# A decoder step's output and gate stages in 512-column chunks, with three row tiles per weight slice

## The reference, cut to what matters

```
o = concat([oa, ob], axis=-1) @ w_out                      # (rows, 2048) @ (2048, 2048)
x = x + _rmsnorm(o, post_w)                                # mean of squares over all 2048 columns
x = x + sigmoid(x @ w_pg + b_pg) * (p @ w_pe)              # gate (2048 x 2048), per-layer input p (256 wide)
```

## Time and profile before

| | us |
|---|---|
| three runs | 4167.61, 4165.46, 4152.4 (median 4165.46) |
| span of the profiled execution | 4170.6 |
| the stage's first matmul to its last | 3133.4 to 4166.0 |
| of these: seven output chunks | 411.0 |
| eighth output chunk, norm and turning | 85.2 |
| eight gate chunks | 536.4 |

### The profile page before, as it was taken

How to read it: one execution, slowest core, us unless ns; L and a number is a source line. 1 busy time by engine, 2 the same in 40 slices (tenths; PEclk the granted TensorE clock), 3 DMA queues, 4 the chain that set the end, 5 groups by cost and what they waited for, 6 DMA issues and landing times. The chain is left out here.

```text
span 4170.6 us, 54158 instructions
## 1 busy us (share of the span) xinstructions
PE 3649.0 (87%) x19483; PEld 2868.8 (69%) x19513; DVE 1942.5 (47%) x3408; ACT 685.9 (16%) x1533; POOL 709.4 (17%) x722
## 2 busy tenths in 40 slices
PE   5969797989898888879789789989979999999999
PEld 3657484857575656658475378778868888888887
DVE  2038686868688989888945311111110000411111
ACT  4010202121111112121200022222220000400000
POOL 2015161615152433325100200000000000000000
PEclk8979798989798988979799879999989999999999
DMA  9865665655565555555510110110040110401012
GB/s 356 249 199 171 206 194 195 205 195 179 199 192 186 186 187 173 163 176 174 187 30 11 46 46 26 35 42 26 6 145 27 40 40 21 136 23 45 23 45 81
DMA packets 355974, 507.28 MB, mean 122 GB/s; under 512 B 58529, under 2 KB 275898, under 8 KB 354546
## 3 DMA queue, kind: packets, MB, share of 16 engines
q1 hardware_dynamic: 312240, 352.67, 27.1%
q0 software_dynamic: 39552, 142.63, 9.8%
q10 hardware_dynamic: 3922, 8.65, 0.5%
HBM read 470.74 MB, written 33.14 MB: 121 GB/s over the span
## 5 line engine op out<-in xcount | busy, mean ns | idle before, releaser
L961 PE MATMUL Z<-W,hT 128*128 128x256 f32 x4096 | 916.6, 386 | 33.2 <-DMA W<-in_w_in_dram 19.7
L961 PEld LDWEIGHTS Z<-W,hT 128*128 128x128 f32 x4096 | 790.1, 194 | 155.4 <-issue 45.7
L1884 PE MATMUL Z<-W,hT 128*128 128x256 f32 x2048 | 456.1, 381 | 4.3 <-PE DB L1895 2.3
L1817 PE MATMUL Z<-W,hT 128*128 128x256 f32 x2048 | 446.9, 381 | 1.3 <-ACT small L1946 1.3
L1884 PEld LDWEIGHTS Z<-W,hT 128*128 128x128 f32 x2048 | 390.6, 191 | 61.1 <-issue 7.7
L1817 PEld LDWEIGHTS Z<-W,hT 128*128 128x128 f32 x2048 | 389.4, 191 | 57.3 <-issue 4.5
L714 POOL TENSOR_TENSOR kprod<-kib,qib 128x256 f32<-128x256 f32 x256 | 348.9, 1372 | 408.1 <-ACT small L802 196.2
L1008 PE MATMUL DB<-big,ex 128*4 128x256 f32 x2048 | 181.8, 488 | 85.8 <-DMA big<-in_cache_diff_v_dram 85.4
L738 POOL DMA_DIRECT2D big<-in_cache_diff_v_dram x256 | 136.4, 533 | 666.3 <-PE DB L1008 533.2
L865 DVE MAX8 small<-big 128x8 f32<-128x512 f32 (+1 forms) x256 | 245.2, 958 | 5.9 <-DVE small L871 1.2
L866 DVE MATCH_REPLACE8 big<-small,big 128x512 f32<-128x512 f32 (+1 forms) x256 | 241.2, 942 | 0.0
(11 more groups left out here) (471 smaller groups left out, 4229.4 us busy)
## 6 DMA issues: line engine op xcount, KB each, us to landing
big<-in_cache_diff_k_dram SPq DMA_DIRECT2D x256, 512.0 KB, 4.3
big<-in_cache_diff_v_dram POOLq DMA_DIRECT2D x256, 512.0 KB, 5.3
W<-in_w_in_dram SPq DMA_DIRECT2D x29, 2048.0 KB
W<-in_w_in_dram SPq DMA_DIRECT2D x48, 1024.0 KB, 7.3
W<-in_w_out_dram SPq DMA_DIRECT2D x8, 2048.0 KB, 8.1
W<-in_w_ple_gate_dram SPq DMA_DIRECT2D x8, 2048.0 KB, 8.4
kib<-in_cache_idx_k_dram SPq DMA_DIRECT2D x256, 32.0 KB
W<-in_x_prompt_dram SPq DMA_DIRECT2D x16, 512.0 KB
```

Source lines behind the costliest of these rows:

```text
L961: mm = pe.matmul(Z[c % 2][:, 0:CW], hT[:, k, t * P:(t + 1) * P], W[:, s, k, :], start=(k == 0), stop=(k == KT - 1))
L1817: mm = pe.matmul(Z[t % 2][:, 0:CW], hT[:, k, t * P:(t + 1) * P], W[:, s, k, :], start=(k == 0), stop=(k == KT - 1))
L1884: pe.matmul(Z[b][:, 0:CW], hT[:, k, t * P:(t + 1) * P], W[:, 1 - s, k, :], start=(k == 0), stop=(k == KT - 1))
```

## The change

- A chunk is now `NQ` = 512 columns: four chunks for each of the two products. Each matmul fills a whole PSUM bank.
- A chunk is done in three groups of three row tiles (`GROUPS`): 0, 1, 2; then 3, 4, 5; then sample rows, 6, 7. Inside a group, the loop over `k` is outside and that over the three row tiles inside. Two sets of three banks (`BANKS`, made of `S` and `Z`) alternate; `TB` and `DB` serve the turning and the per-layer input.
- The weights are a ring of four slices of four `k` (1 MB each). A slice is loaded again as soon as group 2 has used it.
- VectorE takes the tiles out of PSUM, ScalarE squares each 512-column piece at once. Scale and residual go in pieces of 512, in the last three groups of the output part; the residual rows have buffers of their own.
- Tiles 0 to 2 are turned after group 1 of the last output chunk, 3 to 5 after its group 2, the rest after the first group of the gate part.
- Gate: the per-layer matmuls of a group stand in the next group at `k` 3, 6 and 9. Results are stored chunk by chunk. The last group of the program (`last_group`) goes tile by tile.
- The loops of the stage are written out instead of being hardware loops.

```diff
@@ the heads' stage, sync: the first chunk of w_out
-                for c in range(2):
-                    sp.dma_start(W[:, c, :, :], wo[:, :, c * CW:(c + 1) * CW]).then_inc(h_next, 16)
+                for q in range(2):
+                    sp.dma_start(W[:, q, :, :].rearrange("p b c -> p (b c)").rearrange("p (k n) -> p k n", n=512),
+                                 wo[:, 8 * q:8 * q + 8, 0:512]).then_inc(h_next, 16)
@@ the output and gate stage
-        NCO = D // CW
+        NQ = 512
+        NCO = D // NQ
...
+        GROUPS = ((0, 1, 2), (3, 4, 5), (NT, 6, 7))
+        ORDER = ((0, 1, 2), (3, 4, 5), (6, 7, NT))
+        BANKS = ((S[0][:, 0:NQ], S[0][:, NQ:2 * NQ], S[1][:, 0:NQ]), (S[1][:, NQ:2 * NQ], Z[0][:, :], Z[1][:, :]))
+        SIDE = (TB[:, :], DB[:, :])
+        NG = 2 * NCO * 3
...
+                def slices(C, q):
+                    src = (wo if C < NCO else wg)[:, 4 * q:4 * q + 4, (C % NCO) * NQ:(C % NCO) * NQ + NQ]
+                    if C:
+                        if q < 3:
+                            sp.wait_ge(o_wu[q], C)
+                        else:
+                            sp.wait_ge(o_z, 9 * C)
+                    sp.dma_start(Wr[:, 4 * q:4 * q + 4, :], src).then_inc(o_w[q], 16)
+                def residual(n):
+                    t, c = n // 4, n % 4
+                    if n >= 4:
+                        sp.wait_ge(o_xm, n - 3)
+                    src = xp[:, t, c * NQ:(c + 1) * NQ] if t < NT else xs[:, c * NQ:(c + 1) * NQ]
+                    sp.dma_start(xq[c][0:rows(t), :], src).then_inc(o_x[c], 16)
...
+                def store(c, g):
+                    for j, t in enumerate(ORDER[g]):
+                        sp.wait_ge(e_y, 9 * c + 3 * g + j + 1)
+                        dst = yp[:, t, c * NQ:(c + 1) * NQ] if t < NT else ys[:, c * NQ:(c + 1) * NQ]
+                        sp.dma_start(dst, oq(t, c)).then_inc(e_st, 16)
...
+                for C in range(1, NCO):
+                    for q in range(4):
+                        slices(C, q)
+                for n in range(4 * 3):
+                    residual(n)
+                for q in range(2):
+                    slices(NCO, q)
+                for n in range(4 * 3, 4 * 6):
+                    residual(n)
+                for q in range(2, 4):
+                    slices(NCO, q)
+                for n in range(4 * 6, 4 * (NT + 1)):
+                    residual(n)
+                gate_vectors(0)
+                gate_vectors(1)
+                for c in range(NCO):
+                    store(c, 0)
+                    if c + 1 < NCO:
+                        slices(NCO + c + 1, 0)
+                        slices(NCO + c + 1, 1)
+                    store(c, 1)
+                    if c + 1 < NCO:
+                        slices(NCO + c + 1, 2)
+                        slices(NCO + c + 1, 3)
+                    store(c, 2)
+                    if c + 2 < NCO:
+                        gate_vectors(c + 2)
...
+                def one(gi, t, k):
+                    mm = None
+                    if k == 0 and gi >= 2:
+                        pe.wait_ge(o_zf, 3 * (gi - 2) + ORDER[gi % 3].index(t) + 1)
+                    b = bank(gi, t)
+                    if t < NT:
+                        mm = pe.matmul(b, hT[:, k, t * P:(t + 1) * P], Wr[:, k, :], start=(k == 0), stop=(k == KT - 1))
+                    else:
+                        g = k % 4
+                        mm = pe.matmul(b[32 * g:32 * g + 32, :], odec[:, k, :], Wr[:, k, :], start=(k < 4), stop=(k >= KT - 4))
+                    if k == KT - 1:
+                        mm.then_inc(o_z, 1)
+                    elif gi % 3 == 2 and k % 4 == 3 and t == GROUPS[2][2]:
+                        mm.then_inc(o_wu[k // 4], 1)
+                def rows_sum(gi):
+                    C = gi // 3
+                    pe.wait_ge(o_pc, 2 * C + 2)
+                    for h in range(2):
+                        mm = pe.matmul(bank(gi, NT)[0:NB, 256 * h:256 * h + 256], sel, part[h], start=(h == 0), stop=(h == 1))
+                    mm.then_inc(o_ps, 1)
...
+                        pe.wait_ge(e_m, u - 1)
+                    for k in range(2):
+                        lhs = xst[k][:, t * P:(t + 1) * P] if t < NT else psT[:, k, :]
+                        mm = pe.matmul(SIDE[u % 2][0:rows(t), :], lhs, wpe[c % 2][:, k, :], start=(k == 0), stop=(k == 1))
+                    mm.then_inc(e_p, 1)
+                def group(gi):
+                    for k in range(KT):
+                        if gi % 3 == 0 and k % 4 == 0:
+                            pe.wait_ge(o_w[k // 4], 16 * (gi // 3 + 1))
+                        for t in GROUPS[gi % 3]:
+                            one(gi, t, k)
+                        if k == 2 and gi % 3 == 0 and gi and gi != 3 * NCO:
+                            rows_sum(gi - 1)
+                        if gi > 3 * NCO and k in (3, 6, 9):
+                            ple(gi - 1, k // 3 - 1)
+                def last_group(gi):
+                    for t in GROUPS[gi % 3]:
+                        for k in range(KT):
+                            one(gi, t, k)
+                            if t == NT - 2 and k in (3, 6, 9):
+                                ple(gi - 1, k // 3 - 1)
+                        if t == NT - 2:
+                            rows_sum(gi)
+                    for j in range(3):
+                        ple(gi, j)
+                def turn(t, n):
+                    pe.wait_ge(o_xm, 4 * t + 4)
+                    if t < NT:
+                        for f in range(4):
+                            m = n + f
+                            if m >= 2:
+                                pe.wait_ge(o_tf, m - 1)
+                            for k in range(4):
+                                mm = pe.transpose(SIDE[m % 2][:, k * P:(k + 1) * P], oq(t, f)[:, k * P:(k + 1) * P], ident[:, :])
...
+                for gi in range(3 * NCO):
+                    group(gi)
+                    if gi >= 3 * NCO - 2:
+                        for t in ORDER[(gi - 1) % 3]:
+                            turn(t, 4 * t)
+                rows_sum(3 * NCO - 1)
+                group(3 * NCO)
+                for t in ORDER[2]:
+                    turn(t, 4 * t)
+                for gi in range(3 * NCO + 1, NG - 1):
+                    group(gi)
+                last_group(NG - 1)
...
+                for gi in range(3 * NCO):
+                    if gi % 3 == 2:
+                        sample(gi)
+                    last = gi == 3 * NCO - 1
+                    for t in ORDER[gi % 3][0:2]:
+                        square(gi, t)
+                    if last:
+                        for t in ORDER[1]:
+                            turn(t, 4 * t)
+                    square(gi, ORDER[gi % 3][2])
+                    if gi >= 3 * NCO - 3:
+                        roots(gi % 3)
+                    if gi == 3 * NCO - 2:
+                        for t in ORDER[0]:
+                            turn(t, 4 * t)
+                for t in ORDER[2]:
+                    turn(t, 4 * t)
+                for gi in range(3 * NCO, NG):
+                    if gi % 3 == 2:
+                        sample(gi)
+                    for t in ORDER[gi % 3]:
+                        gate(gi, t)
...
+                def normal(g):
+                    dve.wait_ge(o_sq, 9 * (NCO - 1) + 3 * g + 3)
+                    dve.tensor_reduce(rs9[:, 3 * g:3 * g + 3], ss4[:, 3 * g:3 * g + 3, :], AX.X, ALU.add).then_inc(o_sm, 1)
+                    dve.wait_ge(o_rt, g + 1)
+                    link(dve.reciprocal(rs9[:, 3 * g:3 * g + 3], rs9[:, 3 * g:3 * g + 3]))
+                    for t in ORDER[g]:
+                        r = rows(t)
+                        for c in range(4):
+                            dve.scalar_tensor_tensor(out=oq(t, c), in0=oq(t, c), scalar=rs9[0:r, t:t + 1], in1=postq(c)[0:r, :],
+                                                     op0=ALU.mult, op1=ALU.mult).then_inc(o_nm, 1)
+                            dve.wait_ge(o_x[c], 16 * (t + 1))
+                            dve.wait_ge(o_nm, 4 * t + c + 1)
+                            dve.tensor_tensor(oq(t, c), oq(t, c), xq[c][0:r, :], ALU.add).then_inc(o_xm, 1)
+                dve.wait_ge(o_post, 32)
+                for gi in range(3 * NCO):
+                    for t in ORDER[gi % 3]:
+                        dve.tensor_copy(oq(t, gi // 3), take(gi, t)).then_inc(o_zf, 1)
+                    if gi >= 3 * NCO - 3:
+                        normal(gi % 3)
...
+                    for j, t in enumerate(ORDER[gi % 3]):
+                        u, r = 9 * c + 3 * (gi % 3) + j + 1, rows(t)
+                        b = sg[(u - 1) % 2][0:r, :]
+                        src = take(gi, t)
+                        if u >= 3:
+                            dve.wait_ge(e_y, u - 2)
+                        dve.tensor_tensor(b, src, bgate[c % 2][0:r, :], ALU.add).then_inc(e_a, 1)
+                        dve.wait_ge(e_a, u)
```

(44 more changed lines are left out.)

247 lines of the change are left out of this document (86 added, 161 removed).

## The result

| | before | after |
|---|---|---|
| median of the runs, us | 4164.85 | 4246.15 |
| span of the profiled execution | 4170.6 | 4242.7 |
| first row-tile matmul of the stage | 3133.38 | 3124.75 |
| from there to the end of the span ("the stage") | 1037.22 | 1117.95 |

One run of the changed kernel took 7596 us and one of e5_spread 9258 us, both far outside all others, and every ratio and median here is without them. The ratio is 1.0204, with a 95% interval of 1.0181 to 1.0228, that is 75 to 95 us. The medians are 81.3 us apart, where 89.5 were forecast, and in the two profiled executions the stage became 80.7 us longer. What lies ahead of it differs between executions of the same code (the stage's first matmul stands between 3113 and 3133 us in the traces of this study), so for the experiments I give the stage as well as the median.

A forecast was written before the change was run, and what follows sets the result against it. TensorE's own work was taken as the bound; -3.9 + 103.1 - 11.7 - 2.7 + 3 + 1.7 = +89.5 us on the median 4165.5 gave 4255. Own range 4240 to 4270; 8 in 10: 4216 to 4278.

The forecast's parts named there:

- wide matmuls: Row tiles of both parts: a 512-column pass takes 1.99 times as long as a 256-column one; -3.9 us.
- sample rows: Seven interleaved chunks: each narrow pass streams alone and pays for changes of weight width; +103.1 us.
- sums: Copy and summing matmul of the sample rows: deferred into the next group, TensorE waits less; -11.7 us.
- seam: Between output and gate parts: three places of transposes alone, 24.1 us in sum instead of 26.8; -2.7 us.
- clock: Granted TensorE clock at the seam: three transposing places instead of one; +3 us, between 0 and 6.
- tail: Last pass to end of span: VectorE works off two 512-column tiles, 6.3 us instead of 4.6; +1.7 us.
- round trip: TensorE's change from 128 to 32 weight columns and back, around sample-row passes; about 0.30 us each.
- free round trip: Rival: changing between 32 and 128 weight columns costs nothing in this order; 37 us less, 4218; chance 0.10.
- overlap: Rival: sample passes still run beside other passes, so sample rows stay near 30.6 us; 4152; chance 0.07.
- The thin cover: VectorE's scaling of tiles 3 to 5 ends near +55, group 2 near +56; a few us at most.

The follow-up runs named there:

- e5_spread: e6_row_residual with the turning spread under the matmuls of the last output chunk's group 2 and the first gate group; 4132.4 us, ratio 0.9915 to the kernel before.
- e7_halves: Changed kernel with each row tile's 512-column matmul issued as two of 256 into halves of the same bank; 4249.7 us.
- e3_wide: Changed kernel, same order, with 128 instead of 32 weight columns for each sample-row matmul (sample rows not computed rightly); 4226.1 us.
- e6_row_residual: e1_row with the residual rows of tiles 3 to 5 ahead of the gate part's first two weight slices in SyncE's queue; 4141.8 us, ratio 0.9938.
- e4_before_mixed: Kernel before, with the sample rows' sixteen matmuls between those of row tile 7 in the first seven output chunks; 4239.4 us, ratio 1.0166.
- e1_row: Changed kernel with the sample rows' sixteen matmuls in a row at the start of group 2; 4151.1 us, ratio 0.9964 to the kernel before.

## Why the prediction was right

The forecast and its mechanism held; the change cost 81.3 us by the medians, 8 us less than the 89.5 of the sum, and nearly all of this is the clock. By the steps:

| step | forecast | measured | where |
|---|---|---|---|
| wide matmuls | -3.9 | -5.4 | stage of the run with two halves |
| sample rows | +103.1 | +104.0 | 7 x 16 x (2.89 - 1.72) + 3.6 - 30.6 |
| sums | -11.7 | -11.7 | 8 x 1.16 + 1.2 left of 22.2: a sum takes 0.96, the pass behind it 0.2 more; the 1.2 is the forecast's |
| seam | -2.7 | -0.5 | breaks of 10.3, 9.5, 6.5 |
| clock | +3 | -5.2 | below |
| tail | +1.7 | +0.7 | below |

The column gives 81.9 us, against the 80.7 of the stage and the 81.3 of the medians. The remaining microsecond stays open.

**The sample rows** were sized from two single changes and one alternating stage; that estimate, 0.30 a round trip, measured 0.315. The stage that alternated with 2 columns had shown 0.28; whether VectorE has a part in that row no run tests. Both rivals that turned on this term fell with one row each: 2.89 us a `k`, neither 2.58 (free round trip) nor 1.72 (overlap). The fixed cost per matmul as the Trainium skill has it (TensorE: Matmul & The Clock Gate, "Wait — 56ns, not 53.3ns?") fits the steps between passes of one kind: 2.5 ns for each pass more in e7_halves. It doesn't cover a change of kind, which costs 0.315 us a round trip. There the Trainium skill's TensorEngine Tiling (Array Packing), "Key Properties", has the engine drain, and the runs agree: the price came with the narrow columns in the old kernel too (0.31) and went with them in e3_wide.

**The seam** was 2.2 us longer than its sum. In the chain of the first break ScalarE's copies start 2.0 us after the last wide pass (2.1 were forecast), but the fours of transposes then take up to 0.95 us, not 0.67:

```profile
3598.80 0.49 ACT hT L1983
...
3599.33 0.67 PE TB L1924 x4
...
3600.77 0.92 PE TB L1924 x4
3601.68 0.85 PE DB L1924 x4
3602.54 0.95 PE TB L1924 x4
```

That is the clock, below. In the second break VectorE was the late one, by less than a microsecond: it finished the scaling at 3653.4 and took out tiles 6 and 7 behind it, where group 2 ended at 3653.2. With the residual rows earlier (e6_row_residual) the same break is 8.8 us instead of 9.5:

```profile
3652.68 0.69 DVE qkT L2050
3653.37 0.61 DVE e L2055
```

**The clock** is the term that came out wrong, in sign. I forecast +3 us for more slow passes, since there are three breaks instead of one. Measured are -3.2, because the first gate tile is no longer slow, and -2.0 at the start of the stage, which the forecast had not looked at. About 1.1 us of clock stand in the seam's row instead: the first break took 10.3 us, and 9.3 in the runs in which it ran at full clock. Busy time and granted clock of the changed kernel in the three breaks and behind them:

```profile
core 0: us, PE busy (x) PEld busy (x) DVE busy (x) ACT busy (x) POOL busy (x), PEclk, DMA share, GB/s
3596.00:3607.00 11.00, 8.85 (x51) 6.38 (x50) 2.44 (x5) 8.53 (x18) 0.00 (x0) 0.84 0.00 0
3607.00:3618.00 11.00, 11.00 (x25) 3.22 (x24) 0.00 (x0) 0.60 (x1) 0.00 (x0) 1.00 0.00 0
3652.00:3663.00 11.00, 7.99 (x53) 5.54 (x53) 2.46 (x4) 7.54 (x17) 0.00 (x0) 1.00 0.71 242
...
3704.00:3712.00 8.00, 6.92 (x53) 5.04 (x52) 0.16 (x1) 4.78 (x10) 0.00 (x0) 1.00 0.01 2
```

The clock fell once, inside the first break, to 0.84 on its mean (a stretch at 1.2 GHz, the rest at 2.4), and was back before group 2. None of the three ended in slow wide matmuls. In the old seam TensorE was busy 13 of 20 us with gaps; here it was busy 7 to 9 of 8 to 11 us, the wide passes at the windows' edges among them. In these traces three short breaks were kinder than a long one; which property of them makes it so is not tested. Which break the clock falls in is not fixed either: in e7_halves, with the same three breaks, it was the second (0.61 from 3663 to 3667 us), and there too it was 1.00 again before the wide matmuls.

Besides, the old kernel's stage began at half clock in its trace and lost 2 us there, this one's didn't. That varies between executions of one kernel: the first trace of e6_row_residual began at 1.00 and the second at 0.50. But the old order began at 0.50 in both of its traces (the kernel before and e4_before_mixed), and the new one in two of nine, so whether the 2 us are chance alone stays open.

**The tail.** The end of the program, chain of waits:

```profile
4194.68 3.57 PE Z L1861 x32
...
4218.30 13.93 PE Z L1858 x32
4232.23 1.73 PE DB L1888 x4
...
4238.09 0.68 DVE ex L2068
...
4240.17 0.68 DVE vnew L2075
```

From the last wide pass to the end of the span, 4232.2 to 4242.7, are 10.5 us; I had 5.2 + 6.3. Without the 5.2 of the last three per-layer pairs that is 5.3, against 4.6 before. The first line is the last chunk's sample rows in a row, 3.57 us, as forecast 3.7.

**The thin cover** of VectorE's scaling under group 2 was forecast as ending at +55 against +56 after group 1, and it ended at +56.6 against +56.4. But I priced only what it costs in this kernel. The experiment that took the main loss away (e1_row) showed what it costs without that cover, 11 us.

## What to carry to other kernels

Before matmuls of unlike weight width are interleaved, read two things from the trace: whether the narrow ones run at once where they are (many passes within the length of one), and the start-to-start step at the change. In this kernel interleaving lost the first wholly (18.7 us a chunk instead of 3.6) and paid the second each time; with like weight widths, transposes included, it was free. After removing a loss, look again at every work that the lost time had covered.

## What the runs showed that I had not expected

- Wide passes of 512 columns don't hide the change either: the step into narrow columns is 0.09 us over a plain one and out of them 0.09 again plus 0.1 for the unhidden load, at 256 and at 512 columns alike (0.31 and 0.315 a round trip). A pass ahead that is twice as long doesn't make the change cheaper.
- Transposes alone can hold the granted clock up, and bring it back. In e6_row_residual it stayed at 1.00 through all three breaks, with TensorE busy 6.3 of 9.1, 6.4 of 8.6 and 5.9 of 7.0 us. In the changed kernel's first break it was 0.53 from 3602 to 3604.5 us, with TensorE busy throughout, and 1.00 from there to 3607, still among transposes. It did fall in one break of the changed kernel and of e7_halves, so that it holds is not certain.
- The order of loads in SyncE's queue cost under a microsecond in the changed kernel, and 11 us once another loss was removed.
